# Folding the modulation sums of a two-block transformer kernel: TensorE transposes replaced by VectorE block transposes, row sums and four small products

## The chip, the core and the metric

The kernel runs on one core of one Trainium2 chip, in one launch. The metric is the device time of that core in microseconds. Three runs of the kernel before took 1431.91, 1433.44 and 1435.62 us, so the median is 1433.44 us. PE is TensorE (PEld its weight loads), DVE is VectorE, ACT is ScalarE, SP is the queue that issues nearly all DMAs.

## The reference, cut to what matters

The program is two layers of a hybrid attention block and then two layers of a second block, on 256 tokens of width 1024. The second block is modulated by a vector that depends only on the input `c`:

```
c_act = jax.nn.silu(c)                       # (1, 1024)
for l in range(2):
    mod = c_act @ w_ada[l] + b_ada[l]        # w_ada[l]: (1024, 6144)
    sh1, sc1, g1, sh2, sc2, g2 = jnp.split(mod, 6, axis=-1)
    h = modulate(rmsnorm(x, norm1[l]), sh1, sc1)
    ...                                       # projection, retention, pooling, w_out
    x = x + g1 * (merged @ w_out[l])
    h2 = modulate(rmsnorm(x, norm2[l]), sh2, sc2)
    ...
    x = x + g2 * ((silu(gate) * up) @ w_ffn_out[l])
```

The first block (two layers: projection, three kinds of attention, `w_out`, an MLP of width 4096) doesn't use `mod`. So the 2 x 6144 sums over 1024 products can be made at any time before the second block needs them.

## The kernel before, in words

Every large weight goes the same way. SP loads a slab of 512 KB into one of eight buffers `raw`, ACT copies it to `w_hi` (a rounded copy, line 577), DVE makes `w_lo = raw - w_hi` (line 1073), and PE multiplies both parts with the activations' high and low parts (`slab`, lines 1924 to 1930, 24 matmuls of 256 or 258 columns; `slab_both`, lines 1945 and 1946, 16 matmuls of 512 and 256 columns). ACT and DVE make slabs in order, some 5 to 8 slabs ahead of PE; each engine's order is written out by hand, and semaphores connect them. There are 450 slabs.

The stages, in order, are: A0 and A1 (layers 0 and 1 of the first block; each ends in an MLP with an up half of 32 slabs, from about 141 and 451 us, and a down half of 32 slabs, to about 325 and 635 us), P0 (projections, retention and output of the second block's layer 0), F0 (its FFN: an up half of 44 slabs to about 968 us, and a down half of 22), P1 and F1 (the same for layer 1).

The modulation vector is made beside these stages, in 24 groups of 512 columns (`ADA_PLAN`, line 87): groups 0 to 6 in A0's MLP, 7 to 13 in A1's, 14 and 15 in P0, 16 to 19 in F0, 20 and 21 in P1, 22 and 23 in F1. One group is:

1. four DMAs of 512 KB into `ada` (line 427). Load e waits for `ada_sum` to reach e - 2 and stands in the same SP queue as the slabs;
2. eight products on DVE (`ada_product`, lines 1157 and 1163): `ada_acc[g % 2]` gets `ada * cact[k]` added, 128 x 512. They lie at positions that `ADA_PLAN` gives, counted in slabs p of the stage;
3. `ada_sums(g)` on PE, 4 positions after the last product: four transposes of 128 x 128 (line 1977) into `mx[:, 0]`;
4. `ada_columns(g)` on DVE, 6 positions after the last product: a row sum over PSUM, 128 x 512 to 128 x 4 (line 1171), and the addition of the bias into `modT` (line 1172).

In A0 and A1 the last products of the groups lie at p = 12, 21, 30 (up half) and 37, 43, 49, 56 (down half, d = 5, 11, 17, 24 of its 32 slabs); so `ada_columns` in the down half lies at d = 4, 11, 17, 23 and 30. In F0 the last products lie at p = 16, 29, 42 and 55, `ada_columns` at p = 22, 35, 48 and 61. In F1 they lie at p = 20 and 36.

Two closed rounds over DVE and ACT matter beside this:

- The down half of an MLP (loop over d, lines 1558 to 1580): after every fourth slab DVE makes a tile of the residual (lines 1572 to 1574, `x_ready`); ACT then makes `h` and a square from it (lines 602 and 607) and only then the next `w_hi`, three to five of them; DVE's next `w_lo` waits for the first.
- The up half of the FFN (loop over u, lines 1859 to 1878): DVE scales the gate and the up part (1864, 1867), ACT makes silu and two `w_hi`, DVE makes `w_lo`, the product (1871), the `ada` products of this u, another `w_lo`, and `u_lo` (1877). PE starts the last part of its first output chunk only when `u_lo` of u = 21 is there.

Of the kernel before, what the change touches and what calls it, by code (L numbers as in the profile page):

```python
# [23 lines left out]
ALU = mybir.AluOpType  # L24
AX = mybir.AxisListType.X
ds = bass.ds

P = 128
# [95 lines left out]

ADA_DONE = (0, 0, 7, 7, 14, 16, 20, 22, 24)

# [72 lines left out]
def program(nc, consts, x, ln1, w_in, conv_w, conv_b, igate_b, fgate_b, mlstm_norm, moba_q_norm, moba_k_norm,  # L199
# [4 lines left out]
    with ctx:  # L204
# [38 lines left out]
        head_eps = sb("head_eps", [P, 1])  # L243
        ada_part = sb("ada_part", [P, 4])
        few = sb("few", [P, 16])
# [97 lines left out]
        ada_landed = [sem(f"ada_landed{j}") for j in range(3)]  # L343
        ada_sum = sem("ada_sum"); ada_col = sem("ada_col"); ada_out = sem("ada_out")
        s_con = sem("s_con"); s_con2 = sem("s_con2"); s_x = [sem(f"s_x{n}") for n in range(2)]
# [718 lines left out]
        def _(dve):  # L1064
# [79 lines left out]
            def ada_product(q):  # L1144

                e, part = divmod(q, 2)
                g, k = divmod(q, 8)
                o = ada_acc[:, g % 2]
                if q == 0:
                    dve.wait_ge(c_silu, 1)  # L1150
                if part == 0:
                    dve.wait_ge(ada_landed[e % 3], 16 * (e // 3) + 16)
                w = cact[:, k:k + 1]
                if k == 0:
                    if g >= 2:
                        dve.wait_ge(ada_col, g - 1)
                    ins = V.tensor_scalar(o, ada[:, e % 3, 0], w, None, ALU.mult)
                else:
                    if part == 0:
                        dve.wait_ge(ada_sum, e)  # L1160
                    else:
                        ca.wait(ca.n)
                    ins = V.scalar_tensor_tensor(o, ada[:, e % 3, part], w, o, ALU.mult, ALU.add)  # L1163
                if part:
                    ins.then_inc(ada_sum, 1)
                else:
                    ca.done(ins)

            def ada_columns(g):
                dve.wait_ge(ada_col, g + 1)  # L1170
                ca.link(V.tensor_reduce(ada_part[:], mx[:, 0].rearrange("p (n k) -> p n k", n=4), AX, ALU.add))
                V.tensor_tensor(modT[:, 4 * g:4 * g + 4], ada_part[:], vecT[:, V_BADA + 4 * g:V_BADA + 4 * g + 4],
                                ALU.add).then_inc(ada_out, 1)

            def beside(stage):
                tiles, columns = ada_tiles(stage), ada_sums_at(stage, 6)

                def work(p):
                    for q in tiles.get(p, ()):
                        ada_product(q)  # L1180
                    if p in columns:
                        ada_columns(columns[p])
                return work
# [16 lines left out]
            def rest_of_vectors():  # L1200
                dve.wait_ge(boot_t, 6)
                boot.done(V.tensor_scalar(vecT[:, V_LN2:V_C], acc[:, 3, V_LN2:V_C], float(D) ** 0.5, None, ALU.mult))
                V.tensor_copy(vecT[:, V_C:P], acc[:, 3, V_C:P]).then_inc(vec_ready, 1)
# [378 lines left out]
            for l in range(LAYERS):  # L1582
# [135 lines left out]
                ada_product(8 * g0 + 7)  # L1718
                to_sbuf(8, 9)
                lo_upto(p0 + 15)  # L1720
                to_sbuf(10)
# [9 lines left out]
                lo_upto(p0 + 20)  # L1731
                ada_columns(g0 + 0)
                rope2(3)
# [13 lines left out]
                ada_product(8 * g0 + 14)  # L1747
                ada_product(8 * g0 + 15)
                to_sbuf(22)
                decayed(1)  # L1750
                to_sbuf(23)
                ada_columns(g0 + 1)
                to_sbuf(24)
# [165 lines left out]
        def _(pe):  # L1919
# [51 lines left out]

            def ada_sums(g):
                pe.wait_ge(ada_sum, ADA_UNITS * (g + 1))
                if g >= 1:
                    pe.wait_ge(ada_out, g)
                for n in range(4):
                    ins = nc.tensor.transpose(mx[:, 0, n * P:(n + 1) * P], ada_acc[:, g % 2, n * P:(n + 1) * P], ident)
                ins.then_inc(ada_col, 1)
# [34 lines left out]
            for l in range(LAYERS):  # L2013
# [279 lines left out]
                up_slab(3)  # L2293
                sums = ada_sums_at(("A", l), 4)

                def ada_after(p):
                    if p in sums:
                        ada_sums(sums[p])

# [23 lines left out]
            for l in range(LAYERS):  # L2323
# [96 lines left out]
                g0 = ADA_PLAN["P", l][0]  # L2420
                project(0, 1, 2, 3, 4, 5, 6, 7, 8, 9, 10, 11, 12)
                pe.wait_ge(n_var, l * 2 + 5)
                ada_sums(g0 + 0)
                project(13, 14, 15, 16)
                values2(0)
                project(17, 18)
                pe.wait_ge(ada_out, g0 + 1)
                ret_scores(0)
# [5 lines left out]
                pe.wait_ge(b_p, l * 8 + 1)  # L2434
                ada_sums(g0 + 1)
                project(25)
# [61 lines left out]

                sums = ada_sums_at(("F", l), 4)

                def ada_after(p):
                    if p in sums:
                        ada_sums(sums[p])

# [59 lines left out]
```

## Time and profile before

| what | value |
|---|---|
| median of three runs | 1433.44 us (1431.91 to 1435.62) |
| the profiled execution, its own time | 1434.96 us |
| its span | 1433.1 us |
| PE busy | 1407.3 us, 98% |
| DVE busy | 1145.7 us, 80% |
| ACT busy | 828.5 us, 58% |
| mean DMA rate | 207 GB/s |
| chain that ended last | PE 77%, DVE 11%, ACT 6%, issue 3%, DMA 2% |

The span is the stretch between the first and the last instruction of the profiled execution; its own time has 1.9 us more around it. A PE that is busy 98% of the time is one whose matmuls follow each other without a gap; the chain of work says what released each step. Starts of consecutive rows on one engine give the pitch, which is shorter than the duration of one where instructions overlap in the pipeline.

### The profile page before, as it was taken

Reading aid. Unit: us, or ns where it says so; the run is one execution under the profiler, and the core shown is the slowest. Engines: PE = TensorE matmul, PEld = TensorE weight load, DVE = VectorE, ACT = ScalarE, POOL = GpSimd, SP = SyncE. Lnnn points to the kernel's source line nnn. Section 1 sums busy time; section 2 is a strip of 40 time slices with the busy share of each in tenths; the row PEclk is TensorE's granted clock in tenths of the full one; section 3 lists DMA queues with packets and bytes.
Section 4 is the critical chain, followed back from the end, with each engine's and each line's share of the span. In section 5 each row is a group of like instructions: output and inputs, shape, how many; then the busy total and the mean of one; then the engine's idle time right before and its main releaser. Section 6 shows DMA issues by size and latency. Waiting matters only on the chain.

```text
span 1433.1 us, 25543 instructions
## 1 busy us (share of the span) xinstructions
PE 1407.3 (98%) x10339; PEld 1312.1 (92%) x10339; DVE 1145.7 (80%) x1799; ACT 828.5 (58%) x1249; POOL 10.5 (1%) x21
## 2 busy tenths in 40 slices
PE   8999999999999999999999999999999999999997
PEld 7898888889888888889999999998899999999986
DVE  7898888889798888887778777777777787778763
ACT  6776776445776875343666555444446575554542
POOL 2000000000000000000000000000000000000000
PEclk9999999999999999999999999999999999999999
DMA  9643999985445999987854578798787556778662
GB/s 257 161 140 92 284 266 268 299 229 163 137 140 169 278 259 295 284 248 217 226 153 144 172 233 233 212 250 231 225 235 217 148 147 180 231 208 232 180 186 64
DMA packets 485364, 297.13 MB, mean 207 GB/s; under 512 B 14956, under 2 KB 455792, under 8 KB 485120
## 3 DMA queue, kind: packets, MB, share of 16 engines
q1 hardware_dynamic: 483728, 292.00, 71.0%
q8 instruction: 83, 1.36, 0.4%
q0 software_dynamic: 704, 1.66, 0.4%
q10 hardware_dynamic: 816, 1.84, 0.3%
q14 instruction: 33, 0.27, 0.1%
HBM read 289.43 MB, written 1.05 MB: 203 GB/s over the span
## 4 chain that ended last, share of the span: by engine, by line
PE 77%; DVE 11%; ACT 6%; issue 3%; DMA 2%; SPq 1%; DVEq 0%; ACTq 0%
PE acc L1928 12%; PE acc L1929 12%; PE acc L1930 12%; PE mx L1945 9%; PE acc L1945 8%; PE mx L1946 5%; DVE w_lo L1073 4%; PE acc L1946 4%; DVE ada_acc L1163 2%; ACT w_hi L577 2%; PE acc L1960 1%; PE acc L1961 1%; PE acc L1962 1%; DMA rotb<-projb 1%; PE mx L2363 1%
## 5 line engine op out<-in xcount | busy, mean ns | idle before, releaser
L1073 DVE TENSOR_TENSOR w_lo<-raw,w_hi 128x1024 fp32r<-128x1024 f32 x450 | 541.5, 1220 | 113.3 <-ACT w_hi L577 111.4
L577 ACT ACTIVATE w_hi<-raw 128x1024 fp32r<-128x1024 f32 x450 | 458.2, 1049 | 137.7 <-DMA raw<-in_w_in 83.5
L1928 PE MATMUL acc<-h,w_hi 128*128 128x258 f32 (+1 forms) x1776 | 508.6, 286 | 8.4 <-DVE projb L1591 3.4
L1929 PE MATMUL acc<-h,w_hi 128*128 128x258 f32 (+1 forms) x1776 | 503.7, 284 | 0.0
L1930 PE MATMUL acc<-h,w_lo 128*128 128x258 f32 (+1 forms) x1776 | 498.0, 280 | 0.0
L1928 PEld LDWEIGHTS acc<-h,w_hi 128*128 128x128 f32 x1776 | 335.0, 189 | 15.7 <-issue 4.8
L1930 PEld LDWEIGHTS acc<-h,w_lo 128*128 128x128 f32 x1776 | 338.3, 190 | 0.0
L1929 PEld LDWEIGHTS acc<-h,w_hi 128*128 128x128 f32 x1776 | 335.9, 189 | 2.6 <-issue 2.4
L1945 PE MATMUL mx<-u,w_hi 128*128 128x512 f32 x864 | 303.4, 396 | 0.1
L1946 PE MATMUL mx<-u,w_lo 128*128 128x256 f32 x864 | 240.8, 279 | 0.0
L1945 PEld LDWEIGHTS mx<-u,w_hi 128*128 128x128 f32 x864 | 162.0, 188 | 37.1 <-DVE u L1877 0.4
L1945 PE MATMUL acc<-h,w_hi 128*128 128x512 f32 x512 | 181.2, 397 | 0.9 <-issue 0.9
L1946 PEld LDWEIGHTS mx<-u,w_lo 128*128 128x128 f32 x864 | 162.8, 188 | 0.0
L1946 PE MATMUL acc<-h,w_lo 128*128 128x256 f32 x512 | 143.6, 280 | 0.0
L1163 DVE SCALAR_TENSOR_TENSOR ada_acc<-ada,cact,ada_acc 128x512 f32<-128x512 f32 x168 | 125.5, 747 | 2.6
L1945 PEld LDWEIGHTS acc<-h,w_hi 128*128 128x128 f32 x512 | 96.7, 189 | 24.1 <-issue 1.5
L1946 PEld LDWEIGHTS acc<-h,w_lo 128*128 128x128 f32 x512 | 96.5, 188 | 0.1
L1043 ACT ACTIVATE gt<-gt 128x256 f32<-128x256 f32 x44 | 22.4, 510 | 85.8 <-DVE gt L1864 85.8
L1928 PE MATMUL acc<-y,w_hi 128*128 128x256 f32 x224 | 63.4, 283 | 0.0
L1930 PE MATMUL acc<-y,w_lo 128*128 128x256 f32 x224 | 63.0, 281 | 0.0
L1929 PE MATMUL acc<-y,w_hi 128*128 128x256 f32 x224 | 63.0, 281 | 0.0
L602 ACT ACTIVATE h<-xT,nx 128x256 fp32r<-128x256 f32 x16 | 8.2, 510 | 73.1 <-DVE xT L1574 42.8
(294 smaller groups left out, 1649.1 us busy)
## 6 DMA issues: line engine op xcount, KB each, us to landing
raw<-in_w_in SPq DMA_DIRECT2D x132, 512.0 KB, 4.0
ada<-in_w_ada SPq DMA_DIRECT2D x96, 512.0 KB, 5.0
raw<-in_w_ffn_in SPq DMA_DIRECT2D x88, 512.0 KB, 4.9
raw<-in_w_up SPq DMA_DIRECT2D x64, 512.0 KB, 5.6
raw<-in_w_down SPq DMA_DIRECT2D x64, 512.0 KB, 5.9
raw<-in_w_out SPq DMA_DIRECT2D x32, 512.0 KB, 3.9
raw<-in_w_ffn_out SPq DMA_DIRECT2D x32, 512.0 KB, 4.2
raw<-in_w_ret_o SPq DMA_DIRECT2D x16, 512.0 KB, 3.8
```

Source lines behind the costliest of these rows:

```text
L577: nc.scalar.activation(w_hi[:, n % NS], raw[:, n % NS], ACT.Copy).then_inc(hi_ready, 1)
L1043: nc.scalar.activation(gt[:, u % 2, 0:S], gt[:, u % 2, 0:S], ACT.Silu, bias=gt[:, u % 2, S:W - 1]).then_inc(g_silu, 1)
L1073: V.tensor_tensor(w_lo[:, n % NS], raw[:, n % NS], w_hi[:, n % NS].bitcast(F32), ALU.subtract).then_inc(lo_ready, 1)
L1163: ins = V.scalar_tensor_tensor(o, ada[:, e % 3, part], w, o, ALU.mult, ALU.add)
L1928: mm(outp, w_hi[:, i % NS, k], rhs[:, k, 0], start=k == 0, stop=False)
L1929: mm(outp, w_hi[:, i % NS, k], rhs[:, k, 1], start=False, stop=False)
L1930: ins = mm(outp, w_lo[:, i % NS, k], rhs[:, k, 0], start=False, stop=k == KT - 1)
L1945: mm(halves(bank), w_hi[:, i % NS, j], part, start=first, stop=False)
L1946: return mm(bank[:, S:], w_lo[:, i % NS, j], part[:, 0], start=False, stop=last)
L1960: mm(o, w_hi[:, i % NS, n], hi, start=first and n % 2 == 0, stop=False)
L1961: mm(o, w_hi[:, i % NS, n], lo, start=False, stop=False)
L1962: return mm(o, w_lo[:, i % NS, n], hi, start=False, stop=last and n % 2 == 1)
```

## The change

Steps 3 and 4 of a group are replaced. Right behind a group's last product DVE makes `ada_turned(g)`: a block transpose of `ada_acc[:, 0]` into `ada_acc[:, 1]` (each 32 x 32 block turned in its place, 128 x 512), then a row sum over each block, 128 x 512 to 128 x 16, kept in `ada_rows` for the group. Both are linked by a wait, and so is the transpose to the last product. `ada_acc` has one accumulator now instead of two; the next group's first product waits for the row sum. At four places (`ADA_FOLDS`: groups 0 to 6 in A1 at slab 8 of the MLP, 7 to 15 in P0, 16 to 21 in P1, 22 and 23 in F1 behind slab 39) PE makes four products of 128 x 32 weights (`ada_fold`) with 8 to 36 columns, each into 32 partitions of `mx[:, 0]`, and DVE adds the bias of all those groups in one instruction of 128 x 8 to 128 x 36. The PE waits for `ada_out` at the norms (`ADA_DONE`) move accordingly. One row sum of the identity at the start makes `ada_fold`.

```diff
-ADA_DONE = (0, 0, 7, 7, 14, 16, 20, 22, 24)
+ADA_FOLDS = ((0, 7), (7, 9), (16, 6), (22, 2))
+FOLD_A, FOLD_F = 8, 39
+ADA_DONE = (0, 0, 0, 0, 7, 16, 16, 22, 24)
...
-                o = ada_acc[:, g % 2]
+                o = ada_acc[:, 0]
...
-                    if g >= 2:
-                        dve.wait_ge(ada_col, g - 1)
+                    if g >= 1:
+                        dve.wait_ge(ada_row, g)
...
-            def ada_columns(g):
-                dve.wait_ge(ada_col, g + 1)
-                ca.link(V.tensor_reduce(ada_part[:], mx[:, 0].rearrange("p (n k) -> p n k", n=4), AX, ALU.add))
-                V.tensor_tensor(modT[:, 4 * g:4 * g + 4], ada_part[:], vecT[:, V_BADA + 4 * g:V_BADA + 4 * g + 4],
-                                ALU.add).then_inc(ada_out, 1)
+            def ada_turned(g):
+
+                n = [at <= g < at + count for at, count in ADA_FOLDS].index(True)
+                dve.wait_ge(ada_sum, ADA_UNITS * (g + 1))
+                if n:
+                    dve.wait_ge(ada_col, n)
+                ca.link(V.transpose(ada_acc[:, 1], ada_acc[:, 0]))
+                V.tensor_reduce(ada_rows[:, g - ADA_FOLDS[n][0]].rearrange("p n m -> p (n m)"),
+                                ada_acc[:, 1].rearrange("p (b k) -> p b k", b=16), AX, ALU.add).then_inc(ada_row, 1)
+
+            def ada_columns(n):
+                at, count = ADA_FOLDS[n]
+                dve.wait_ge(ada_col, n + 1)
+                V.tensor_tensor(modT[:, 4 * at:4 * (at + count)], mx[:, 0, 0:4 * count],
+                                vecT[:, V_BADA + 4 * at:V_BADA + 4 * (at + count)], ALU.add).then_inc(ada_out, count)
...
                     for q in tiles.get(p, ()):
                         ada_product(q)
-                    if p in columns:
-                        ada_columns(columns[p])
+                        if q % 8 == 7:
+                            ada_turned(q // 8)
+                    if (*stage, p) == ("A", 1, FOLD_A + 2):
+                        ada_columns(0)
+                    if (*stage, p) == ("F", 1, FOLD_F + 2):
+                        ada_columns(3)
...
+                boot.done(V.tensor_reduce(ada_fold[:], ident.rearrange("p (a k) -> p k a", a=4), AX, ALU.add))
...
                 to_sbuf(8, 9)
+                ada_turned(g0)
                 lo_upto(p0 + 15)
...
-                ada_columns(g0 + 0)
                 rope2(3)
...
                 ada_product(8 * g0 + 15)
+                ada_turned(g0 + 1)
                 to_sbuf(22)
...
-                ada_columns(g0 + 1)
+                ada_columns(1 + l)
...
-            def ada_sums(g):
-                pe.wait_ge(ada_sum, ADA_UNITS * (g + 1))
-                if g >= 1:
-                    pe.wait_ge(ada_out, g)
-                for n in range(4):
-                    ins = nc.tensor.transpose(mx[:, 0, n * P:(n + 1) * P], ada_acc[:, g % 2, n * P:(n + 1) * P], ident)
+            def ada_sums(n):
+
+                at, count = ADA_FOLDS[n]
+                pe.wait_ge(ada_row, at + count)
+                for m in range(4):
+                    ins = mm(mx[32 * m:32 * (m + 1), 0, 0:4 * count], ada_fold[:], ada_rows[:, 0:count, :, m], start=True, stop=True)
                 ins.then_inc(ada_col, 1)
...
-                project(0, 1, 2, 3, 4, 5, 6, 7, 8, 9, 10, 11, 12)
-                pe.wait_ge(n_var, l * 2 + 5)
-                ada_sums(g0 + 0)
-                project(13, 14, 15, 16)
+                project(0, 1, 2, 3, 4, 5, 6, 7, 8, 9, 10, 11, 12, 13, 14, 15, 16)
                 values2(0)
                 project(17, 18)
-                pe.wait_ge(ada_out, g0 + 1)
+                pe.wait_ge(n_var, l * 2 + 5)
...
                 pe.wait_ge(b_p, l * 8 + 1)
-                ada_sums(g0 + 1)
+                ada_sums(1 + l)
```

## Rows read from the trace of the kernel before

**Rows 1.** Windows, core 0: span of time, then busy us of each engine, clock, DMA

```profile
546.00:637.00 91.00, 91.00 (x539) 80.02 (x538) 75.60 (x114) 38.28 (x54) 0.00 (x0) 1.00 1.00 290
```

**Rows 2.** Timeline of PE round the first group's transposes: start us, us

```profile
190.17 0.40 PE L1945 MATMUL acc<-h,w_hi 128*128 128x512 f32 x1
190.41 0.28 PE L1946 MATMUL acc<-h,w_lo 128*128 128x256 f32 x1
190.53 0.60 PE L1977 MATMUL mx<-con,ada_acc 128*128 128x128 f32 x4
190.88 0.48 PE L1945 MATMUL acc<-h,w_hi 128*128 128x512 f32 x1
191.19 0.28 PE L1946 MATMUL acc<-h,w_lo 128*128 128x256 f32 x1
```

**Rows 3.** Timeline of PE, two runs of small matmuls

```profile
133.87 0.88 PE L2138 MATMUL mx<-pT,vtok 128*64 128x128 f32 x12 [0.18 <-ACT pT L758]
...
1425.45 1.05 PE L2538 MATMUL mx<-con,ssq 128*128 128x1 f32 x8 [0.38 <-DVE ssq L1109]
```

**Rows 4.** Groups by form, DVE, two lengths of row

```profile
L1073 DVE TENSOR_TENSOR w_lo<-raw,w_hi 128x1024 fp32r<-128x1024 f32 x450 | 541.5, 1220 | 113.3 <-ACT w_hi L577 111.4
...
L1543 DVE TENSOR_TENSOR ru<-acc,sqt 128x512 f32<-128x512 f32 x32 | 22.1, 690 | 13.4 <-ACT sqt L876 13.3
```

**Rows 5.** Chain of waits in A1's down half: start us, us, what

```profile
599.79 0.66 DVE ada_acc L1163
...
601.50 0.76 DVE ada_acc L1163
...
603.04 0.61 DVE ada_part L1171
```

**Rows 6.** Timeline of DVE, one `ada_columns` and the product behind it

```profile
203.58 0.68 DVE L1171 TENSOR_REDUCE ada_part<-mx 128x4 f32<-128x512 f32 x1
...
204.38 0.74 DVE L1163 SCALAR_TENSOR_TENSOR ada_acc<-ada,cact,ada_acc 128x512 f32<-128x512 f32 x1
```

**Rows 7.** Timeline of DVE, the first waits of the down halves, and a later one

```profile
244.85 1.23 DVE L1073 TENSOR_TENSOR w_lo<-raw,w_hi 128x1024 fp32r<-128x1024 f32 x1 [0.47 <-ACT w_hi L577]
...
312.42 1.23 DVE L1073 TENSOR_TENSOR w_lo<-raw,w_hi 128x1024 fp32r<-128x1024 f32 x1 [1.90 <-ACT w_hi L577]
...
555.28 1.23 DVE L1073 TENSOR_TENSOR w_lo<-raw,w_hi 128x1024 fp32r<-128x1024 f32 x1 [0.87 <-ACT w_hi L577]
```

**Rows 8.** Timeline of DVE at the ends of the down halves of A0 and A1

```profile
324.62 0.68 DVE L1171 TENSOR_REDUCE ada_part<-mx 128x4 f32<-128x512 f32 x1
...
325.66 0.42 DVE L1572 TENSOR_TENSOR ru<-mx,sqt 128x256 f32<-128x256 f32 x1 [0.16 <-ACT sqt L890]
...
635.35 0.68 DVE L1171 TENSOR_REDUCE ada_part<-mx 128x4 f32<-128x512 f32 x1
...
636.14 0.42 DVE L1572 TENSOR_TENSOR ru<-mx,sqt 128x256 f32<-128x256 f32 x1
```

**Rows 9.** Timeline of PE: slab 92 in A0, and where P0 begins

```profile
316.47 0.48 PE L1945 MATMUL mx<-u,w_hi 128*128 128x512 f32 x1
...
638.67 0.39 PE L1928 MATMUL acc<-h,w_hi 128*128 128x258 f32 x1 [1.32 <-DVE h L1100]
```

**Rows 10.** Groups by form, DVE's scaling of the gate in F0 and F1

```profile
L1864 DVE TENSOR_TENSOR gt<-acc,rstd 128x258 f32<-128x258 f32 x44 | 18.5, 421 | 0.1
```

**Rows 11.** Timeline of PE in F0, at its first output chunk's last part

```profile
975.06 0.28 PE L1946 MATMUL mx<-u,w_lo 128*128 128x256 f32 x1
975.41 0.50 PE L1945 MATMUL mx<-u,w_hi 128*128 128x512 f32 x1
```

**Rows 12.** Timeline of DVE in F1's up half

```profile
1308.72 0.43 DVE L1867 TENSOR_TENSOR upv<-acc,rstd 128x258 f32<-128x258 f32 x1 [0.75 <-PE acc L1930]
```

**Rows 13.** Timeline of DVE in P0, chunks 11 and 12 leave PSUM

```profile
679.92 0.76 DVE L1591 TENSOR_TENSOR projb<-acc,rstd 128x258 f32<-128x258 f32 x2
```

**Rows 14.** Timeline of PE in P0, the first matmul of slab 15

```profile
683.28 0.28 PE L1928 MATMUL acc<-h,w_hi 128*128 128x258 f32 x1
```

More of the change, by code:

```diff
@@ L243, in program @@
         head_eps = sb("head_eps", [P, 1])
-        ada_part = sb("ada_part", [P, 4])
+        ada_fold = sb("ada_fold", [P, 32])
+        ada_rows = sb("ada_rows", [P, 9, 4, 4])
         few = sb("few", [P, 16])
@@ L343, in program @@
         ada_landed = [sem(f"ada_landed{j}") for j in range(3)]
-        ada_sum = sem("ada_sum"); ada_col = sem("ada_col"); ada_out = sem("ada_out")
+        ada_sum = sem("ada_sum"); ada_row = sem("ada_row"); ada_col = sem("ada_col"); ada_out = sem("ada_out")
         s_con = sem("s_con"); s_con2 = sem("s_con2"); s_x = [sem(f"s_x{n}") for n in range(2)]
@@ L1167, in ada_product @@
                     ca.done(ins)
-            def ada_columns(g):
-                dve.wait_ge(ada_col, g + 1)
-                ca.link(V.tensor_reduce(ada_part[:], mx[:, 0].rearrange("p (n k) -> p n k", n=4), AX, ALU.add))
-                V.tensor_tensor(modT[:, 4 * g:4 * g + 4], ada_part[:], vecT[:, V_BADA + 4 * g:V_BADA + 4 * g + 4],
-                                ALU.add).then_inc(ada_out, 1)
+            def ada_turned(g):
[11 more added lines that the diff above has]
+                                vecT[:, V_BADA + 4 * at:V_BADA + 4 * (at + count)], ALU.add).then_inc(ada_out, count)
             def beside(stage):
-                tiles, columns = ada_tiles(stage), ada_sums_at(stage, 6)
+                tiles = ada_tiles(stage)
                 def work(p):
@@ L2293, in _ @@
                 up_slab(3)
-                sums = ada_sums_at(("A", l), 4)
                 def ada_after(p):
-                    if p in sums:
-                        ada_sums(sums[p])
+                    if (l, p) == (1, FOLD_A):
+                        ada_sums(0)
                 pe.wait_ge(n_var, l * 2 + 2)
@@ L2497, in _ @@
                 out_slab(7)
-                sums = ada_sums_at(("F", l), 4)
                 def ada_after(p):
-                    if p in sums:
-                        ada_sums(sums[p])
+                    if (l, p) == (1, FOLD_F):
+                        ada_sums(3)
                 for s in range(FFN_IN):
```

## The prediction

> **What bounds the kernel now.** I read the table of engines first: PE is busy 98% of the span, which seems to make this simple, since the change takes work from PE. The windows show the same by stage: in A1's down half PE is busy for 91.00 of 91 us and DVE for 75.60 [rows 1], and F0's up half looks alike. So the end of the kernel is set by how fast PE gets through its queue, as long as the others stay ahead of it. The second question is by how much they do, and a busy share doesn't answer that. I took it from the timelines, as the distance between the end of a slab's `w_lo` and PE's first matmul on it, and from what ends DVE's idle time.
>
> In the down halves DVE's waits name ACT's `w_hi` and not PE: 1.90 us at 312.42, once in each round of four slabs [rows 7]. That is the closed round residual tile, `h`, square, `w_hi`, `w_lo`; no PE is in it, and such a round lasts longer than PE's four slabs. So DVE starts each down half well ahead and loses ground: its lead at the seventh round is 2.8 us in A0 (slab 92 is split at 312.42 + 1.23 = 313.65 and used at 316.47) [rows 7, 9], and by the same reading 1.9 us in A1. In F0's up half DVE waits for PE in neither of its scalings; for the gate the idle time is 0.1 us over all 44 instructions [rows 10]. That too is a round of DVE and ACT, 5.62 us with one `ada` product in it against 5.72 us of PE for two slabs. At its end PE already waits for `u_lo` of u = 21: two matmuls that should be 0.12 us apart start at 975.06 and 975.41 [rows 11]. So these three stretches are balanced between PE and a DVE round, and what is added to DVE there is not hidden.
>
> **The change part by part.**
>
> PE loses the transposes. Four of them start at 190.53 and the next slab matmul at 190.88, 0.35 us; that matmul is followed at 191.19, 0.31 us later, where its like before the transposes took 0.24 (190.17 to 190.41) [rows 2]. Together 0.43 us a group, and all 24 places look alike: 24 x 0.43 = 10.3 us.
>
> PE gains four folds of four fp32 products with 32 columns of weights. An fp32 product is recorded as two matmuls, so a fold has eight. The nearest rows: twelve with 64 weight columns in 0.88 us, eight with 128 in 1.05 [rows 3], which without the last one's own 0.28 or 0.25 us are 0.055 and 0.114 us each. Eight of them are 0.44 to 0.91 us, with 0.08 for the slab behind them 0.5 to 1.0 us. I take 0.7, between the two, so 2.8 us for four. Below zero it can't be, for they are new. The page "TensorE: Matmul & The Clock Gate" of the Trainium skill says under "Why this matters for your kernels" that small products whose outputs lie in different groups of 32 partitions run at the same time; a fold would then be near 0.5 us, and the sum 0.8 us less. The first row, whose outputs alternate between two halves, is the shorter one, so the trace leans that way, but no row has four groups.
>
> DVE loses `ada_columns`: 203.58 to 204.38, 0.80 us [rows 6], 24 times. It gains four additions of some 0.16 us, which I count as nothing (places with 3 us of lead or more), and `ada_turned`, 24 times. Its cost T is the number on which all hangs. The transpose waits for the last product: a product whose successor needs it takes 0.76 us with 0.02 of issue, against 0.66 for one whose successor doesn't [rows 5], so +0.12. The transpose itself is in no row. Long rows show 1220 - 690 = 530 ns for 512 more elements and so 0.16 us fixed [rows 4]; at that rate 512 elements are 0.69 us, as any 128x512 instruction with two inputs. With its link 0.72. The row sum takes 0.61 until the next instruction starts [rows 5]. So T = 0.12 + 0.72 + 0.60 = 1.44 us. Bounds for the transpose: 0.48 us (a first product `ada_acc` of this size) and 1.22 us (as for 1024 elements), so T = 1.2 to 2.0. I take 1.44, since the rate of one element per cycle is what nearly all rows show. The page "VectorE: DVE Perf Modes", "The three transpose paths", has 311 ns for a 128x128 block transpose of 2-byte elements; four of these would be 1.24 us, T = 2.0, and is a rival below. Its rate without a fixed part four times over gives my value, and no row here decides.
>
> DVE over a whole stage: +0.64 us a group net. Where it matters is what stands between two points at which PE or a DMA sets DVE's time anew.
>
> *Down halves of A0 and A1.* Before them PE's up half paces DVE (its row sums wait for PE's pairs). Between the last product of the third group (p = 30) and the first `w_lo` that waited for a `w_hi` from a late DMA, `ada_turned` stands in idle time, of which only 0.47 us (A0) and 0.87 us (A1) are there [rows 7]. From there to the last residual tile come four more (d = 5, 11, 17, 24), and five `ada_columns` go (d = 4, 11, 17, 23, 30). In A0 the last tile began at 325.66, and DVE reached the `ada_columns` ahead of it at 324.62 [rows 8]; now it gets there at 324.62 + 5 x 1.44 - 0.47 - 4 x 0.80 = 328.15, +2.49 us. In A1: 635.35 + 7.20 - 0.87 - 3.20 = 638.48 instead of 636.14 [rows 8], +2.34. The next stage's first slab waits for what follows from this tile (638.67, 1.32 us, DVE `h`) [rows 9], so both go into the time in full. PE's own gain in the down half, five transposes or 2.15 us, is lost entirely: PE waits longer at the end, and already at the slabs of d = 29 and 30: DVE's lead there is 2.8 and 3.2 us in A0, 1.9 and 2.2 in A1, and DVE comes 3.53 (A1: 3.13) us later while PE would come 2.15 earlier. What is kept is that of groups 0 and 1 in the up half, -0.86 us, and in A1 the fold comes on top, +0.7. A0: +1.63. A1: +2.18.
>
> *F0.* Three `ada_turned` (p = 16, 29, 42) and two `ada_columns` less (22, 35) before the last `u_lo`: 3 x 1.44 - 1.60 = +2.72 us on the point 975.41, at which PE stands already [rows 11]. The two transposes that PE loses before it are not seen. Gates leave PSUM with 2.1 us to spare at the worst place, and the same lateness uses just that. In the down half the lead is 5 us or more and one `ada_turned` replaces two `ada_columns`: PE keeps its 0.86. F0: +1.86.
>
> *F1.* From the middle of the up half DVE waits for PE in each u (0.75 us at 1308.72) [rows 12], so 1.44 us once is caught up in two. P0 and P1: the stall of chunk 12 lies before `ada_turned`; behind it chunk 11 leaves PSUM by 680.35 (679.92 and 0.43) [rows 13] for the slab at 683.28 [rows 14], a margin of 2.9 us that shrinks by 1.44 and by 0.43. It holds; if T were above 2.4, it would cost the rest, and then twice. Each of the three stages: -0.86 + 0.7 = -0.16, together -0.48.
>
> *Start and queues.* The row sum for `ada_fold` puts some 0.2 us between evictions at 27 us, taken as 0.1. SP waits for `ada_sum` before its loads; the last product of a group signals ahead of the transpose, so the next load but one is later by T, and slabs stand behind it in the queue. DVE's slabs are later by as much, so I count nothing more.
>
> Sum: 1.63 + 2.18 + 1.86 - 0.48 + 0.1 = +5.3 us. It was made on an execution of 1434.96 us (span 1433.1, 1.9 around it), which is 1.5 above the median; on that execution it is 1440.3, on the median of 1433.44 it is 1438.7. The dependence on T is 5 + 5 + 3 = 13 us for each us.
>
> **The rivals.**
>
> *PE alone counts (faster).* If the rounds of DVE and ACT could take up the lateness, for example because their idle 1.90 us are slack, the change would be worth 24 x 0.43 - 2.8 - 0.1 = 7.4 us: 1426.0. PE's busy 98% speaks for it. Against it: the 1.90 us are released by ACT, whose `h` was waiting for DVE's own tile. It decides at the point where A0's last tile no longer moves. 18%.
>
> *A cheap T.* With the transpose at 0.48 us, T = 1.23: 5.3 - 2.7 = +2.6, 1436.0; or a penalty taken up in one of the three stretches gives about the same. No difference that can be told (0.3%, 4.3 us, is about what a measurement of this kernel can tell). 24%.
>
> *A dear T.* With 1.24 us for the transpose T = 2.0 and 13 x 0.56 = +7.3 more: 1446.0. 4-byte elements through a block transpose might do this; all rows at one element per cycle speak against it. 13%.
>
> *The forecast*, 1437 to 1442: 45%.
>
> **How the numbers follow.** The rivals' distances are 1426.0, 1436.0, 1438.7 and 1446.0. Slower by over 0.3% (above 1437.7): 35 of the forecast's 45 and the dear T, 0.48. Faster by over 0.3% (below 1429.1): most of the first rival, 0.17. The rest 0.35. The range from 1427.5 to 1446 leaves out about half of the first and half of the third rival. The forecast's own range is 1437 to 1442.
>
> **What would show each step.** PE rows: no transposes, four folds of eight short matmuls, 0.4 to 0.9 us each. DVE: transposes of 0.69 us, row sums of 0.68 with 16 results. New waits of PE for `w_lo` at the slabs of d = 29 and 30, together 2.5 us in A0 and 3.1 in A1, and behind them a wait for DVE's `h` that is 2.1 us longer after A0 and 1.4 after A1; a wait of some 3.8 us for `u_lo` at the end of F0's up half, where there were 0.23. A wrong forecast would show as DVE idle in those stretches while PE goes on without a gap, or as a transpose far from 0.69 us.

## The result, and the profile after

The changed kernel takes 1441.27 us (median of 6 runs, 1439.67 to 1446.14), the kernel before, run beside it, 1434.24 us (1431.91 to 1436.79). The ratio on record is 1.0059, 95% interval 1.0046 to 1.0071. So the kernel is slower, clear of the noise: by 7.0 us between the two medians, by 8.5 us if the ratio is taken. The ratio isn't the quotient of the two medians (1.0049), and below it is named beside them where the two differ. The profiled execution took 1439.67 us, its span 1437.8; against the profiled one of before that is only 4.7 us more. Where the other 2.3 us are is a question of its own, below.

First the sizes of what was added. These are groups by form of the changed kernel (line, engine, operation, tiles, count, then busy us and mean ns, then idle time):

```profile
L1178 DVE STREAM_TRANSPOSE ada_acc<-ada_acc 128x512 f32<-128x512 f32 x24 | 17.1, 711 | 0.8
L1179 DVE TENSOR_REDUCE ada_rows<-ada_acc 128x16 f32<-128x512 f32 x24 | 16.5, 686 | 0.8
```

A block transpose of 128x512 is 0.711 us, with the rate of any row of 512 elements as in [rows 4], and not the 1.24 us that would come of taking four times the 311 ns of the Trainium skill ("VectorE: DVE Perf Modes", "The three transpose paths"). That figure is for 128x128 elements of 2 bytes, and four times it is not what 512 columns of 4 bytes cost here. The fold, in PE's timeline between the matmuls of two slabs:

```profile
479.06 0.28 PE L1965 MATMUL acc<-h,w_lo 128*128 128x256 f32 x1
479.27 0.29 PE L1996 MATMUL mx<-ada_rows,ada_fold 128*32 128x28 f32 x8
479.49 0.50 PE L1964 MATMUL acc<-h,w_hi 128*128 128x512 f32 x1
479.83 0.28 PE L1965 MATMUL acc<-h,w_lo 128*128 128x256 f32 x1
```

Eight matmuls in 0.29 us. From 479.06 to 479.49 and on to 479.83 are 0.77 us, where two such steps without a fold take 0.12 and 0.23: the fold costs 0.42 us. By the same reading the folds of P0 and P1 cost 0.44 and 0.40, and that of F1, which has a wait of 0.17 us in it, 0.61.

Then the waits (engine and line, what it waited for, us in total, times, longest), first at the end of A0's down half, then for A1's:

```profile
PE acc L1947 <- DVE h L1103: 2.6, 1, 2.6
PE mx L1964 <- DVE w_lo L1076: 2.4, 3, 1.0
```

The lines for 590:642, at the end of A1, are the same two, 2.6 and 2.4. In before the wait for `h` was 0.5 us after A0 and 1.32 after A1 [rows 9], and there was none for `w_lo`. Why VectorE is behind is in its own timeline and ACT's, in the seventh round of A0:

```profile
309.91 0.42 DVE L1592 TENSOR_TENSOR xT<-ru,xT 128x256 f32<-128x256 f32 x1
312.24 1.23 DVE L1076 TENSOR_TENSOR w_lo<-raw,w_hi 128x1024 fp32r<-128x1024 f32 x1 [1.91 <-ACT w_hi L580]
...
314.89 0.71 DVE L1178 STREAM_TRANSPOSE ada_acc<-ada_acc 128x512 f32<-128x512 f32 x1
315.64 0.69 DVE L1179 TENSOR_REDUCE ada_rows<-ada_acc 128x16 f32<-128x512 f32 x1
316.24 3.48 DVE L1076 TENSOR_TENSOR w_lo<-raw,w_hi 128x1024 fp32r<-128x1024 f32 x3
```

```profile
310.37 0.51 ACT L605 ACTIVATE h<-xT,vecT 128x256 fp32r<-128x256 f32 x1 [7.15 <-DVE xT L1592]
310.78 0.40 ACT L610 ACTIVATE sqt<-xT 128x256 f32<-128x256 f32 x1
311.09 2.95 ACT L580 ACTIVATE w_hi<-raw 128x1024 fp32r<-128x1024 f32 x3
```

ACT stands idle for 7.15 us before the residual tile comes, and the next `w_hi` stands behind that tile's `h` in its queue. So VectorE, once it has made the tile, waits 1.91 us for work that ACT could have done long before. This is the closed round of [rows 7], once for every residual tile. It has no slack, and each pair of new instructions pushes back what stands behind it. PE waits three times for it: at slab d = 25 (0.76 us at 301.49), at d = 29 (0.66 us, for the `w_lo` of 312.24) and at d = 30 (0.95 us, for the first of the three of 316.24, behind the two new instructions).

In F0 the end of the up half, VectorE and then PE:

```profile
975.99 0.48 DVE L1890 SCALAR_TENSOR_TENSOR upv<-upv,gt 128x256 f32<-128x256 f32 x1
976.38 0.75 DVE L1166 SCALAR_TENSOR_TENSOR ada_acc<-ada,cact,ada_acc 128x512 f32<-128x512 f32 x1
977.17 0.71 DVE L1178 STREAM_TRANSPOSE ada_acc<-ada_acc 128x512 f32<-128x512 f32 x1
977.91 0.69 DVE L1179 TENSOR_REDUCE ada_rows<-ada_acc 128x16 f32<-128x512 f32 x1
978.52 0.41 DVE L1896 TENSOR_TENSOR u<-upv,u 128x256 fp32r<-128x256 f32 x1
```

```profile
978.99 0.80 PE L1964 MATMUL mx<-u,w_hi 128*128 128x512 f32 x1 [3.47 <-DVE u L1896]
979.58 0.41 PE L1965 MATMUL mx<-u,w_lo 128*128 128x256 f32 x1
979.79 0.63 PE L1964 MATMUL mx<-u,w_hi 128*128 128x512 f32 x1
```

PE waited 3.47 us for `u_lo` (the same instruction let PE on at 975.41 in before [rows 11]), and the matmuls behind the wait take 0.63 and 0.41 us instead of 0.39 and 0.28. The windows of the same place (span; busy us of PE, its loads, DVE, ACT, POOL; granted clock; DMA share; GB/s) say why:

```profile
970.00:975.00 5.00, 5.00 (x30) 4.38 (x29) 3.80 (x8) 2.21 (x5) 0.00 (x0) 1.00 1.00 259
...
979.00:980.00 1.00, 1.00 (x3) 0.90 (x4) 0.96 (x2) 1.00 (x2) 0.00 (x0) 0.50 0.93 322
980.00:981.00 1.00, 1.00 (x4) 0.81 (x4) 1.00 (x3) 0.23 (x1) 0.00 (x0) 0.50 0.97 311
981.00:982.00 1.00, 1.00 (x5) 0.90 (x4) 1.00 (x2) 0.00 (x0) 0.00 (x0) 0.50 0.86 259
982.00:984.00 2.00, 2.00 (x13) 1.71 (x13) 1.97 (x5) 0.00 (x0) 0.00 (x0) 0.98 1.03 306
```

After the wait the granted clock is 0.50, the 1.2 GHz level, for some 3 us. PE is 3.58 us later than before at 978.99 (975.41 there), and 4.56 at the first matmul of the second slab behind it (979.77 in before, 984.33 here). In between before has four transposes, 0.43 us, and the changed kernel has none. So the half clock costs 4.56 - 3.58 + 0.43 = 1.4 us on top of the wait; experiment 5 shows the same wait without it.

The whole by stages, each the time from PE's first matmul of one slab to that of another, read from PE's timeline. A0 runs from the first slab of its MLP to the second of A1; A1 from the first slab of its own MLP to the second of P0; P0 to the first of F0; F0 to the second of P1; P1 to the second of F1; F1 to the twentieth of the 22 slabs of its down half. Beside the two kernels stand second traces of both (below).

| | before, two traces | changed, two traces | difference of means | forecast |
|---|---|---|---|---|
| A0 | 187.46, 187.56 | 189.40, 189.44 | +1.91 | +1.63 |
| A1 | 188.12, 188.35 | 189.97, 190.35 | +1.93 | +2.18 |
| F0 | 193.45, 193.41 | 196.41, 196.30 | +2.93 | +1.86 |
| F1 | 179.12, 179.12 | 178.88, 178.88 | -0.24 | -0.16 |
| P0 | 200.74, 198.35 | 198.37, 199.16 | -0.8 | -0.16 |
| P1 | 201.97, 205.05 | 203.14, 201.45 | -1.2 | -0.16 |

A0, A1, F0 and F1 repeat within 0.4 us and make +6.5 us, where the forecast had +5.5 for these four. P0 and P1 differ by up to 3 us between two traces of one kernel; with them the six stages make +4.5 us.

### The profile page after: what moved, and what is told of

Same layout as the page of the kernel before. It is cut to its first block, busy times and chain, and to the rows that moved or that the text cites. A ratio compares the mean times of both kernels' runs of the same rounds, so it can differ in the third digit from the quotient of the medians.

```text
span 1437.8 us, 25419 instructions
## 1 busy us (share of the span) xinstructions
PE 1400.4 (97%) x10275; PEld 1304.1 (91%) x10275; DVE 1160.0 (81%) x1804; ACT 827.3 (58%) x1249; POOL 10.5 (1%) x21
## 4 chain that ended last, share of the span: by engine, by line
PE 60%; DVE 22%; ACT 9%; issue 7%; DMA 2%; SPq 1%; DVEq 0%; ACTq 0%
PE acc L1947 9%; PE acc L1948 9%; PE acc L1949 9%; PE acc L1964 8%; DVE w_lo L1076 8%; PE mx L1964 5%; DVE ada_acc L1166 5%; ACT w_hi L580 4%; PE acc L1965 4%; PE mx L1965 3%; ACT gt L1046 1%; DVE upv L1890 1%; PE acc L1979 1%; DMA raw<-in_w_in 1%; PE acc L1981 1%
```

## The experiments

Times of before are those of the runs beside each kernel, on the same chip.

**1 to 4. ScalarE's order, and where the instructions stand.** One edit on ScalarE, put into the kernel before and into the changed one:

```diff
-hi_upto(m0 + min(MLP_UP + 4 * n + 3 + AHEAD, A_MLP + 2))   # down halves
+hi_upto(m0 + min(MLP_UP + 4 * n + 4 + AHEAD, A_MLP + 2))
-hi_upto(at + AHEAD)                                        # FFN, up halves
+hi_upto(at + AHEAD + 1)
```

In the kernel before (1):

> The kernel before, with one thing changed on ScalarE: in the down halves it makes one more w_hi before it waits for the residual tile (bound 4n+4+AHEAD instead of 4n+3+AHEAD), and in the FFN's up halves one more before it waits for the scaled gate. Theory (closed rounds of VectorE and ScalarE): VectorE's idle 1.90 us a round for w_hi in the down halves and 1.19 us a round in F0's up half go, VectorE's lead over PE grows, and as PE is the bound in the kernel before, little comes of it: 1431 to 1434 us against 1434.2. Rival (ScalarE's order is no limit, the idle time is slack or moves to a DMA): the idle time comes back under another name and the time is 1434 or above.

Measured: 1431.93 us (11 runs) against 1432.38; ratio 0.9999 (0.9989 to 1.0008). By stages it gives 0.0 in A0, -0.8 in A1 and -0.65 in F0, too little for the device time to tell. VectorE's waits for `w_hi` fall from 111.4 us to 43.9 over the whole kernel, and those of `upv` for PE grow from 7.6 to 47.7. So its idle time moves to where it waits for PE, as the theory has it: with the rounds open PE ends the stages, and PE's own work was no shorter.

In the changed kernel (2):

> The changed kernel with the same edit on ScalarE. Theory: with the rounds open VectorE takes up 1.44 us a group, PE no longer waits for w_lo in A0 and A1 nor for u_lo in F0 (5.4 and 3.5 us in the changed kernel's trace), and PE's 24 x 0.43 us less four folds of some 0.3 us count in full: 9 us under the kernel before with the same edit, 1422 to 1426 us, so the same change turns from +7 to -9. Rival (VectorE's whole load or the DMAs hold the time, wherever the instructions stand): above 1436 us.

Measured: 1422.49 us (5 runs) against 1432.38; ratio 0.9934 (0.9920 to 0.9949). 9.4 us lie between this kernel and the kernel before with the same edit, measured on the same chip. The same change that costs 7.0 us gains 9.4 once the rounds are open. VectorE's timeline in A1's down half, where it waited some 1.9 us in each round, and at its end:

```profile
608.68 0.43 DVE L1592 TENSOR_TENSOR xT<-ru,xT 128x256 f32<-128x256 f32 x1
609.14 1.22 DVE L1076 TENSOR_TENSOR w_lo<-raw,w_hi 128x1024 fp32r<-128x1024 f32 x1
...
611.80 0.71 DVE L1178 STREAM_TRANSPOSE ada_acc<-ada_acc 128x512 f32<-128x512 f32 x1
612.54 0.69 DVE L1179 TENSOR_REDUCE ada_rows<-ada_acc 128x16 f32<-128x512 f32 x1
...
628.27 0.42 DVE L1590 TENSOR_TENSOR ru<-mx,sqt 128x256 f32<-128x256 f32 x1 [6.49 <-ACT sqt L893]
```

The `w_lo` follows the tile at once, the same two instructions are there, and VectorE has 6.49 us to spare before the last tile, which now follows PE.

The two kernels that take the new instructions away from 13 (3) or from 11 (4) of the groups:

```diff
+if g in (2, 3, 4, 5, 6, 9, 10, 11, 12, 13, 16, 17, 18):    # or: not in
+    V.tensor_copy(ada_rows[...], ada_acc[:, 0, 0:16]).then_inc(ada_row, 1)
+    return
 ca.link(V.transpose(ada_acc[:, 1], ada_acc[:, 0]))
```

> The changed kernel, with block transpose and row sum replaced by a copy of 16 columns (0.17 us) for the 13 groups that are turned after the up halves of A0 and A1 or before F0's last u_lo (2 to 6, 9 to 13, 16 to 18); the modulation of these groups is left out of the computation so. Theory: A0, A1 and F0 keep PE's transposes as gain, -3 us each of the first two and -1.7 us of F0 against before, P0, P1 and F1 as in the changed kernel: 1426 to 1429 us, 14 us under the changed kernel. Rival (each of the 24 turned groups costs alike): the 13 give back 13/24 of what all would, some 8 us: 1433 us.

Measured: 1423.29 us (5 runs), ratio 0.9932 (0.9919 to 0.9946), which is 18 us under the changed kernel's 1.0059 (16 by the medians), where 14 were expected. It lies below the expected range: A0, A1 and F0 give back 3.6, 3.9 and 2.2 us against before, where 3, 3 and 1.7 were named.

> The complement: the same copy in place of block transpose and row sum for the 11 other groups (0, 1, 7, 8, 14, 15, 19 to 23), where VectorE has lead; their modulation is left out of the computation. Theory: no change but for P0 and P1, where a group is turned behind the stall of chunk 12: 1439.5 to 1441.5 us. Rival (each group costs alike): 7 us under the changed kernel, 1434 us.

Measured: 1441.58 us (6 runs), ratio 1.0060 (1.0045 to 1.0075), which is the changed kernel's own, and 18.3 us above the kernel with the thirteen copies, on the same chip. Within the noise the eleven groups outside the rounds cost nothing and the thirteen in them all of it.

**5. The down halves alone.** Only the first of the two edits on ScalarE:

> The changed kernel with ScalarE's edit in the down halves alone; the FFN's up halves stay closed rounds. Theory: A0 and A1 as in the kernel with both edits (1422.5 us), but F0 pays again what it paid in the changed kernel, a wait of 3.5 us for u_lo and 1.1 us at half clock behind it, in all some 5 us: 1427 to 1429 us. Rival (the down halves were all that mattered): 1422 to 1424 us.

Measured: 1429.22 us (10 runs), ratio 0.9970 (0.9957 to 0.9984), just above the theory's range. F0 takes 194.99 us here and 191.02 with both edits, so both places matter. The wait is back:

```profile
PE mx L1964 <- DVE u L1896: 3.5, 1, 3.5
```

But in this trace the clock did not fall behind it, which the expectation had taken for granted. First PE here, then the window of the same place with its granted clock of 1.00, then PE in the changed kernel:

```profile
968.57 0.50 PE L1964 MATMUL mx<-u,w_hi 128*128 128x512 f32 x1 [3.47 <-DVE u L1896]
972.49 0.39 PE L1964 MATMUL mx<-u,w_hi 128*128 128x512 f32 x1
```

```profile
968.00:970.00 2.00, 1.43 (x8) 1.26 (x9) 1.97 (x5) 1.83 (x2) 0.00 (x0) 1.00 0.81 267
```

```profile
984.33 0.39 PE L1964 MATMUL mx<-u,w_hi 128*128 128x512 f32 x1
```

From the end of the wait to the first matmul of the second slab behind it are 3.92 us here and 5.34 in the changed kernel (978.99 to 984.33). The difference, 1.42 us, is the price of the half clock alone. The profiled execution, at 1425.24 us and a mean granted clock of 0.998, is also the shortest of the ten; the others have 0.993 to 0.996 and take 1427.16 to 1433.00 us.

**6. The kernel before without PE's transposes.**

```diff
+if g:
+    mm(mx[0:32, 0, 0:4], ident[:, 0:32], ident[:, 0:4], start=True, stop=True).then_inc(ada_col, 1)
+    return
 for n in range(4):
     ins = nc.tensor.transpose(mx[:, 0, n * P:(n + 1) * P], ada_acc[:, g % 2, n * P:(n + 1) * P], ident)
```

VectorE adds the bias to the bias instead of to the sum.

> The kernel before with PE's four transposes left out for 23 of the 24 groups (one product with 32 columns of weights and 4 of data gives the signal), while VectorE's work is that of before; the modulation is then the bias alone. This is PE's gain by itself. Theory: where a round of VectorE and ScalarE sets the end of the stage (down halves of A0 and A1, F0's up half) nothing comes of it; groups 0, 1, 7, 8, the four of P0 and P1, one in F0's down half and two in F1 count, 11 x 0.43 = 4.7 us less 0.1 each for the product: 1429 to 1431 us against 1433. Rival (PE's work counts everywhere): 23 x 0.33 = 7.6 us, 1425 us or less.

Measured: 1433.46 us (10 runs), ratio 0.9997 (0.9985 to 1.0009). Both missed, and PE's timeline shows a part of why:

```profile
214.09 0.28 PE L1946 MATMUL acc<-h,w_lo 128*128 128x256 f32 x1
214.30 0.23 PE L1977 MATMUL mx<-con 128*32 128x4 f32 x2
214.45 0.50 PE L1945 MATMUL acc<-h,w_hi 128*128 128x512 f32 x1
214.79 0.28 PE L1946 MATMUL acc<-h,w_lo 128*128 128x256 f32 x1
```

From 214.09 to 214.79 are 0.70 us, 0.35 more than without it, for one product of four columns. The four transposes took 0.43, the fold of eight matmuls 0.42. So what PE pays is mostly the interruption of the stream (the switch to other operands and the semaphore waits in it are not told apart), and little of it the work in it: the change gains on PE because it has 4 interruptions instead of 24. As an experiment on PE's gain alone this was a bad one, since it left the interruptions in. It has a second effect too. Behind the first of its products the slabs of A0's, A1's and F0's down halves take 2.83 us, nearly to the end of each, where 2.77 is the pace ahead of it; in before the transposes leave this slower pace behind only in some places. A0, A1, F0 and F1 are together 2.1 us longer than before's. Why the pace changes is open.

**7. PE's part left out altogether**, to mend that:

```diff
 def ada_sums(g):
+    return
...
-dve.wait_ge(ada_col, g - 1)                # ahead of a group's first product
+dve.wait_ge(ada_out, g - 1)
...
-dve.wait_ge(ada_col, g + 1)
-ca.link(V.tensor_reduce(ada_part[:], mx[:, 0].rearrange(...), AX, ALU.add))
+dve.wait_ge(ada_sum, ADA_UNITS * (g + 1))
+ca.link(V.tensor_reduce(ada_part[:], ada_acc[:, g % 2].rearrange(...), AX, ALU.add))
```

> The kernel before with PE's part of the modulation sums left out altogether: no transposes, no product in their place and no wait of PE for them. VectorE's row sum has its old shape (128x512 into 128x4) but reads the accumulator in SBUF and waits for its own last product; the modulation that comes out is not that of the reference. Theory: PE's 0.43 us a group are the price of interrupting the stream of slabs (so that one small product in place of four transposes gave nothing), and they come back only where PE sets the end of the stage: 11 groups outside the closed rounds, 4.7 us, 1428 to 1430 us. Rival (PE's time counts everywhere): 24 x 0.43 = 10.3 us, 1423 us. Second rival (0.43 us a group are not to be had at all): 1433 us.

Measured: 1431.71 us (11 runs) against 1431.37, ratio 0.9999 (0.9990 to 1.0008). By the stages it does what the theory says: A0 186.66 (-0.85 against the mean of before), A1 186.93 (-1.3), F0 192.19 (-1.2), F1 178.94 (-0.2), 3.6 in all; counted from A0's first slab PE reaches the end of A0 3.3 us earlier, and then stands:

```profile
PE acc L1928 <- DVE h L1100: 3.0, 1, 3.0
```

Yet the device time shows none of the 3.6 us, and it lies above the theory's range. P0 and P1 together are not slower here than in the two traces of before (402.25 us against 402.71 and 403.40), but those come from other chips, and there is none of before from this one. The runs of this kernel have a mean granted clock of 0.994 to 0.996, those of before beside them 0.996 to 0.998, and in its trace the clock falls at 672.59 us, 1.1 us behind a wait of 2.04 us, where it doesn't fall in before. Such falls can have taken a part of the 3.6 back; how much isn't shown. It is certain that PE's 10 us alone are not worth 10.

**8. A larger T.** Each block transpose twice:

```diff
+ca.link(V.transpose(ada_acc[:, 1], ada_acc[:, 0]))
 ca.link(V.transpose(ada_acc[:, 1], ada_acc[:, 0]))
```

> The changed kernel with each block transpose made twice, so that VectorE's part of a group lasts 0.73 us more. Theory: 13 us for each us, 9.5 us, and up to 2 us more where PE's longer waits lower its clock as in F0: 1450 to 1453 us. Rival (lateness is taken up by VectorE's idle time once the first wait is there): under 1446 us. If every group counted it would be 24 x 0.73 = 17.5 us, 1459 us.

Measured: 1451.84 us (median of the three runs that agree, 1451.35 to 1454.31; a fourth took 3461.73) against 1433.73, ratio 1.0135 (1.0104 to 1.0167), 11 us over the changed kernel's ratio. That is in the expected range. A0 takes 3.4 us more than in the changed kernel, A1 3.6, F0 2.4: 9.3 in all (unrounded) where 13 x 0.73 = 9.5 were expected. F1 takes 1.5 more, which wasn't: the last fold's products now wait for VectorE, in the middle of PE's queue:

```profile
1364.81 0.25 PE L1997 MATMUL mx<-ada_rows,ada_fold 128*32 128x8 f32 x8 [1.66 <-DVE ada_rows L1180]
```

**9 and 10. The same kernels once more**, for second traces.

> The kernel before, unchanged, for a second trace. It shows how far PE's waits at the start of P0 and P1 (2.53 and 0.90 us before a slab in the first trace, 0.53 and 2.46 in that of the changed kernel), which end with VectorE's work behind the rope copies' landing, scatter in one and the same kernel. If they are chance, they differ here by a us or more; if they belong to the change, they are again about 2.5 and 0.9.

> The changed kernel, unchanged, for a second trace. F0's wait of 3.5 us for u_lo and the half clock behind it should be there again, as should the waits for w_lo and h in A0 and A1; the waits at the start of P0 and P1 should differ from 0.53 and 2.46 us by a us or more in one of the two, as they do between the two traces of the kernel before.

Measured: 1434.63 and 1439.82 us. The stages are in the table above. P0's wait was 2.53 us before and hardly there in the second trace; P1's was 0.90 and then 2.7, and this time the clock fell behind it:

```profile
1062.00:1064.00 2.00, 0.43 (x4) 0.22 (x2) 2.00 (x3) 0.00 (x0) 0.00 (x0) 1.00 0.89 294
1064.00:1066.00 2.00, 0.91 (x4) 0.92 (x5) 2.00 (x5) 0.00 (x0) 0.00 (x0) 0.65 0.46 106
1066.00:1068.00 2.00, 2.00 (x11) 2.00 (x11) 2.00 (x4) 0.00 (x0) 0.00 (x0) 0.50 0.63 166
```

So these waits differ from one execution to the next, with or without the change. In the changed kernel's second trace the waits for `w_lo`, `h` and `u_lo` are all there again (in all 4.9, 5.2 and 3.5 us), and the clock falls once more than in the first, behind the 2.6 us at the end of A1:

```profile
642.00:644.00 2.00, 1.56 (x7) 1.56 (x8) 1.94 (x4) 2.00 (x4) 0.00 (x0) 0.56 0.00 0
644.00:646.00 2.00, 2.00 (x12) 1.97 (x12) 2.00 (x3) 1.90 (x2) 0.00 (x0) 0.59 0.59 155
```

The traces of (4), (8) and (11) keep the changed kernel's waits (in F0 that of (8) is 4.2 us), and in each the clock falls three times: at the end of A0, at the end of A1 and in F0. The waits at the ends of A0 and A1 are 2.6 us in these three traces as in the two of the changed kernel. Counted from the end of the wait, PE is 1.1 to 1.2 us later behind a fall at A0's end, and 1.4 to 1.6 at A1's, than the first trace of the changed kernel, which has no fall there.

**11. The fold in one group of partitions.**

```diff
-ins = mm(mx[32 * m:32 * (m + 1), 0, 0:4 * count], ada_fold[:], ada_rows[:, 0:count, :, m], ...)
+ins = mm(mx[0:32, 0, 128 * m:128 * m + 4 * count], ada_fold[:], ada_rows[:, 0:count, :, m], ...)
```

> The changed kernel with the four products of a fold written to the same 32 partitions at four column offsets, instead of to four groups of 32 partitions; the modulation is then the bias alone. Looked at for PE's rows of the fold: in the changed kernel eight matmuls are recorded as 0.25 to 0.32 us in all. If the four groups run beside each other, the eight last about twice as long or more here, 0.5 to 0.9 us; if they are short because so few columns move, it is again 0.25 to 0.32.

Measured, for the same fold as above:

```profile
479.64 0.59 PE L1996 MATMUL mx<-ada_rows,ada_fold 128*32 128x28 f32 x8
480.16 0.50 PE L1964 MATMUL acc<-h,w_hi 128*128 128x512 f32 x1
```

0.59 us instead of 0.29, for the same eight matmuls. Four groups of 32 output partitions do run beside each other. The whole execution took 1441.68 us (one run).

**12. Rope copies ahead of the `ada` loads**, on the changed kernel with both edits on ScalarE:

```diff
-P_LOADS = (3, 4, 5, 12, 13, 16, 18, 22)
+P_LOADS = (3, 4, 5, 14, 14, 16, 18, 22)
 ada_product(8 * g0 + 5)
-ada_product(8 * g0 + 6)
 lo_upto(p0 + 14)
-ada_product(8 * g0 + 7)
 to_sbuf(8, 9)
+ada_product(8 * g0 + 6)
+ada_product(8 * g0 + 7)
 ada_turned(g0)
```

> The changed kernel with ScalarE's edit in both stages, and in P0 and P1 the two 512 KB ada loads that stood ahead of the first rope copies in SP's queue put behind them; on VectorE chunks 8 and 9 leave PSUM before the two products that use those loads. Theory (PE's waits at the start of P0 and P1 end with the landing of the copies, which queue behind weights): VectorE's wait for the copies falls from 4 to 6 us to 2 to 4, and as PE hardly waits there in the kernel with the edit, the median falls from 1422.5 to 1420.5 to 1422, with less scatter. Rival (the copies' landing is set by something else): the waits for the copies stay, 1422 to 1424 us.

Measured: 1418.82 us (4 runs, 1418.36 to 1419.42) against 1431.37, ratio 0.9907 (0.9892 to 0.9923). It is the fastest of all, and below the expected range. Against the kernel without this edit it gains 2.7 us by the medians, each taken against before beside it, and 3.9 by the ratios; by stages P1 is 1.7 us shorter and P0 0.3, and PE's wait of 1.46 us at P1's start is gone. Its four runs lie within 1.1 us. VectorE's wait for the copies, here and in the kernel without this edit:

```profile
DVE rotb L1615 <- DMA rotb<-projb: 6.5, 2, 3.5
```

```profile
DVE rotb L1615 <- DMA rotb<-projb: 10.0, 2, 5.7
```

The two products that moved on VectorE are part of the edit, so what the loads alone are worth isn't told apart. The chain of work that ended last, by engine, of before, of the changed kernel and of this one:

```profile
PE 77%; DVE 11%; ACT 6%; issue 3%; DMA 2%; SPq 1%; DVEq 0%; ACTq 0%
```

```profile
PE 60%; DVE 22%; ACT 9%; issue 7%; DMA 2%; SPq 1%; DVEq 0%; ACTq 0%
```

```profile
PE 92%; DVE 4%; ACT 3%; issue 1%; DMA 0%; SPq 0%; ACTq 0%; DVEq 0%
```

## Why the prediction was right, point by point

The forecast was +5.3 us, 1438.7 in a range of 1437 to 1442, and the mechanism two closed rounds. Measured are 1441.27 us, +7.0 by the medians, and +6.5 in the four stages that repeat, where the terms for them add up to +5.5. The mechanism was right. That the time is only 0.7 us inside the upper end of the range is in part luck: falls of the clock were in no term, and folds cheaper than assumed took some of that back.

- *PE is not the bound everywhere, though it is busy 98%.* Shown: PE's part left out altogether gave nothing in the device time (7), the rounds opened gave nothing (1), both together, by way of the change, 9.4 us (2). The first rival, that PE alone counts, was wrong for this kernel and is right for the one with the rounds open.
- *PE's gain, 24 x 0.43 us.* Right in sum: with the rounds open, A0, A1, F0 and F1 are 9.0 us shorter than in the same kernel without the change, in 20 of the 24 places and with two folds in them: (9.0 + 0.42 + 0.37) / 20 = 0.49 us a place (F1's fold has no wait there and costs 0.37). What the 0.43 consists of I had not asked; it is mostly the interruption (6), and the slower pace behind some of them isn't in it.
- *Four folds of 0.7 us.* Too dear: 0.42, 0.44, 0.40 and 0.61, 1.9 in all and so 0.9 us less. The record of eight matmuls is 0.25 to 0.32 us. The rule of the Trainium skill that I weighed ("TensorE: Matmul & The Clock Gate", "Why this matters for your kernels") holds here, as (11) shows, and its sum, 0.8 us less, was the better one; I had taken the middle between two rows, of which neither had four groups.
- *T = 1.44 us.* From 314.11, where the last product begins, to 316.24 are 2.13 us, less the 0.66 of a product: 1.47. The transpose is 0.71 for a forecast 0.69. The slope of 13 us for each us held in A0, A1 and F0 (9.3 of 9.5), and the dear and the cheap T both fell. One remark of the prediction was wrong: the 311 ns taken four times, with the fixed 0.16 us of [rows 4] counted once, give 0.76 us and not the 0.69 that I took.
- *A0 and A1.* +1.91 and +1.93 for +1.63 and +2.18; A1's fold was 0.28 us cheaper than its term. The waits for `h` grew by 2.1 and 1.3 us, where 2.1 and 1.4 were named. Those for `w_lo` are 2.4 and 2.4 for 2.5 and 3.1, but not all where they were named: 1.6 us of each at d = 29 and 30, and 0.8 at d = 25, which the prediction did not see.
- *F0.* +2.93 for +1.86: this is the term that was mis-sized. Counted from F0's first slab, the point at which PE stood moved by 2.75 us, for a forecast 2.72, and the wait for `u_lo` was 3.5 us, near the 3.8 of the text. But behind it PE ran at 1.2 GHz for 3 us, which cost 1.4 us more. I had priced the wait and not what a PE that has stood can pay behind it. Without this F0 is +1.5, and with the wait but no fall of the clock (5) it is 194.99 against 193.43, +1.6.
- *P0, P1.* The margin behind chunk 12 held. But that the waits at the stages' start scatter by 3 us in one kernel I could not see from one trace, and it is larger than any of my terms.
- *The 2.3 us between the profiled pair and the medians.* The first trace of before had 3.4 us of waits at the starts of P0 and P1, that of the changed kernel 3.0 and one fall of the clock; the other runs of the changed kernel have a mean clock of 0.992 to 0.996 and are the longer the lower it is (1446.14 us at 0.992). The later traces with the same waits have two or three falls instead of one, and each further one costs 1.1 to 1.6 us (10), so two more would make some 2.3 us. That the slower runs of the changed kernel had them is argued, not shown: they have no trace.

## What to carry to other kernels

A busy share of 98% does not make an engine the bound where another pair of engines closes a round: look at what stands in the queue of the engine that the round waits for. Here ACT idled 7 us ahead of an operation that it had put in front of a ready one, and moving one call decided whether 10 us of saved PE time were lost or won. Count an interruption of PE's stream as one price, whatever is in it: join small products before making them cheaper. And where a change makes PE stand for some us, give the clock a term of its own.

## What the hardware showed that I had not expected

- One product of 4 columns between two slabs costs PE 0.35 us, four transposes of 128 columns 0.43, eight fold matmuls 0.40 to 0.44.
- Behind such an interruption the slabs of a down half can go on at 2.83 us each instead of 2.77, until the next one or to the end (6).
- Behind an idle time of PE the granted clock can fall from 1.00 to 0.50 for some 3 us, which cost 1.1 to 1.6 us where it could be compared. The same wait of the same length does it in one execution and not in another: 3.47 us in F0 did in the changed kernel and not in (5), 2.6 us at the end of A1 did in the second trace of the changed kernel and not in the first. In (7) PE stood 2.99 us at the ends of A0 and A1 without a fall.
- With two loads of 512 KB behind small copies in SP's queue instead of ahead of them (12) the time is 2.7 us less by the medians and 3.9 by the ratios. The four runs lie within 1.1 us, the five of the kernel without this within 3.7; with so few runs that the scatter fell is only likely.
